# Modulation computed by blocks of 128 channels, the first two projection tiles summed channel block by channel block, and later roundings of the output weights

## The reference

```python
shift, scale, gate = jnp.split(jax.nn.silu(mod) @ p['ada_w'] + p['ada_b'], 3, -1)
h = rms_norm(x, p['g_pre']) * (1.0 + scale) + shift
z = h @ p['w_in']                      # 1024 -> 4096
... three branches: gated conv, conv module, bidirectional RWKV-7 scan
out = jnp.concatenate([ya, yb, yc], -1) @ p['w_out']
x = x + gate * rms_norm(out, p['g_post'])
```

## Time and profile before

| | us |
|---|---|
| median of 3 runs (lowest, highest) | 1085.96 (1084.84, 1086.45) |
| profiled execution | 1087.09 |
| its span | 1085.3 |

### The profile page before, as it was taken

The page is one execution under the profiler, slowest core; times in us unless marked ns, Lnnn a source line. Parts: engine busy times, 40 slices in busy tenths (PEclk is TensorE's granted clock), DMA queues, the critical chain, the costliest instruction groups (busy, mean ns, idle before and its releaser), DMA issues. The chain is left out here.

```text
span 1085.3 us, 31987 instructions
## 1 busy us (share of the span) xinstructions
PE 1005.1 (93%) x14375; PEld 907.3 (84%) x14375; DVE 641.6 (59%) x952; ACT 426.4 (39%) x708; POOL 409.3 (38%) x372
## 2 busy tenths in 40 slices
PE   5699999999999999994699999999999998899997
PEld 3399999999989888983699999999999997566685
DVE  5351059776457302245688888888888885546532
ACT  5361102100124332222355655666555665434311
POOL 8111112311205312322446555566676665512200
PEclk9699999999999999996699999999999999999999
DMA  9711422111122110000000000000000004421331
GB/s 356 268 37 62 178 84 79 40 39 39 39 83 81 42 39 1 1 1 11 1 4 4 4 4 4 4 4 5 4 4 4 4 4 159 135 109 35 121 117 59
DMA packets 30564, 61.46 MB, mean 57 GB/s; under 512 B 3368, under 2 KB 21972, under 8 KB 29276
## 3 DMA queue, kind: packets, MB, share of 16 engines
q1 hardware_dynamic: 30428, 59.42, 15.5%
HBM read 49.68 MB, written 9.73 MB: 55 GB/s over the span
## 5 line engine op out<-in xcount | busy, mean ns | idle before, releaser
L681 PE MATMUL ps<-input_rounded,weights_rounded 128*128 128x386 f32 x768 | 264.0, 344 | 4.1 <-DVE input_rest L788 2.8
L683 PE MATMUL ps<-input_rounded,weights_rest 128*128 128x386 f32 x768 | 260.7, 339 | 0.0
L682 PE MATMUL ps<-input_rest,weights_rounded 128*128 128x386 f32 x768 | 260.4, 339 | 0.0
L1464 POOL TENSOR_TENSOR arena<-arena,lvl 128x512 f32<-128x512 f32 x108 | 138.8, 1300 | 78.2 <-ACT arena L1372 46.4
L470 POOL TENSOR_TENSOR weights_rest<-arena,weights_rounded 128x2048 fp32r<-128x2048 f32 x16 | 75.8, 4737 | 211.2 <-ACT weights_rounded L515 211.2
L681 PEld LDWEIGHTS ps<-input_rounded,weights_rounded 128*128 128x128 f32 x768 | 145.1, 189 | 10.9 <-issue 7.5
L682 PEld LDWEIGHTS ps<-input_rest,weights_rounded 128*128 128x128 f32 x768 | 145.3, 189 | 0.5
L683 PEld LDWEIGHTS ps<-input_rounded,weights_rest 128*128 128x128 f32 x768 | 145.4, 189 | 0.0
L1157 PE MATMUL ps<-arena 64*64 64x64 f32 x2880 | 107.0, 225 | 18.1 <-issue 14.6
L1157 PEld LDWEIGHTS ps<-arena 64*64 64x64 f32 x2880 | 95.2, 138 | 23.8 <-issue 17.1
L1167 PE MATMUL ps<-arena 64*64 64x64 f32 x2880 | 104.9, 223 | 5.4 <-DVE arena L1595 4.1
(11 more groups left out here) (247 smaller groups left out, 1700.8 us busy)
## 6 DMA issues: line engine op xcount, KB each, us to landing
arena<-in_w_in SPq DMA_DIRECT2D x16, 1024.0 KB, 5.2
arena<-in_ada_w SPq DMA_DIRECT2D x7, 1024.0 KB, 5.3
mix_scratch<-zc SPq DMA_DIRECT2D x4, 1158.0 KB, 9.7
out<-arena SPq DMA_DIRECT2D x9, 512.0 KB, 2.6
zc<-in_x_sample SPq DMA_DIRECT2D x4, 1024.0 KB, 9.1
hT<-in_ada_w SPq DMA_DIRECT2D x4, 1024.0 KB, 12.1
zc<-in_w_out SPq DMA_DIRECT2D x4, 1024.0 KB, 8.6
arena<-in_x_sample SPq DMA_DIRECT2D x8, 512.0 KB, 3.7
```

The source lines that it names most:

```text
L681: pe.matmul(o, w_hi[:, k, cut], hi_of_h[:, k, cols_b], start=(k == 0), stop=False)
L682: pe.matmul(o, w_hi[:, k, cut], lo_of_h[k][:, cols_b], start=False, stop=False)
L683: last = pe.matmul(o, w_lo[:, k, cut], hi_of_h[:, k, cols_b], start=False, stop=(k == KT - 1))
L1464: pool.tensor_tensor(Um[l % 3], UT, lvl[:, l, :].unsqueeze(1).to_broadcast([P, 2 * PAIRS, C]), ALU.mult).then_inc(q_um[l], 1)
```

## The change

- `load_ada(k)` now loads output block k: the 128 shift columns and the 128 scale columns of all 1024 input rows, as two DMAs with runs of 512 bytes. `modulate(k)` sums all eight input blocks for these 256 outputs at once (eight matmuls of 256 columns in four partition groups), `copy_rows(k)` on ScalarE copies the result from PSUM, and `turn(k)` on TensorE sums the four groups and transposes them by two matmuls with a selection matrix. The bias is added per channel in `scale_and_shift(k)`; shift and scale biases are loaded with the small vectors.
- SP's order: x, vectors, ada block 0, first weights, ada blocks 1 to 7, gate rows, LoRA weights.
- The roots take mean and epsilon in the activation, without VectorE, and follow each group's squares. Tile 5 is evicted by VectorE, tile 4 by ScalarE.
- Tiles 0 and 1 sum over channel blocks: for the first six (`TOGETHER`) channel blocks, both tiles and all three column blocks in six banks of PSUM, with the modulation of block k + 2 ahead of block k's products; then the last two channel blocks for tile 0, then for tile 1. `full`, `round_inputs` and `rest` go by channel block, VectorE taking the first two column blocks and ScalarE modulating the third.
- The first weights are rounded in four pieces, the first after block 0's rows, the others behind the first channel blocks; the second weights behind channel block 5. GpSimd makes the rests of the four pieces, and builds the small constants early.
- `round_w_out`: part 0 goes to the place that part 1 had, 1 to that of 2, 2 to that of 3, and 3 behind `copy_y(n3, 4)` of the next step, the last one.

The core of the diff (lines shifted left):

```diff
 GROUPS = ((0,), (1, 2), (3, 4), (5, 6), (7, 8))
-H_CUTS = [(n, k) for n in range(NB) for k in range(KT)]
-EVICT_BY = [1, 1, 1, 1, 1, 0, 0, 0, 0]
+EVICT_BY = [1, 1, 1, 1, 0, 1, 0, 0, 0]
 X_SLOTS = 3
 BY_ACT = 2
+TOGETHER = KT - 2
+CHUNKS = 4
+CHUNK = PIECE // CHUNKS
...
 def load_ada(k):
-    sp.dma_start(ada_at[k], ada_w[0, k * P:(k + 1) * P, 0:2048]).then_inc(s_al[k], 16)
+    for s in range(2):
+        at = D_MODEL * s + P * k
+        sp.dma_start(ada_at[k].rearrange("p (m s n) -> p s m n", m=KT, s=2)[:, s],
+                     ada_w[0, :, at:at + P].rearrange("(m p) n -> p m n", p=P)).then_inc(s_al[k], 16)
...
+load_ada(0)
+load_z(0)
+for k in range(1, KT):
+    load_ada(k)
...
+def early():
+    for n, e in enumerate((RMS_EPS, LN_EPS, KK_EPS, GN_EPS)):
+        pool.memset(epst[:, n:n + 1], e)
+    link(pool.memset(select, 0.0))
+    for b in range(4):
+        link(pool.affine_select(out=select, in_=select, compare_op=ALU.not_equal, fill=1.0, base=-32 * b,
+                                pattern=[[-1, 2]], channel_multiplier=1))
+    for v in (kkT, lo2):
+        for a in (0, TS - 2, W - 2):
+            last = pool.memset(v[:, 0:4, a:a + 2], 0.0)
+    last.then_inc(s_const, 1)
...
+def split_first(c):
+    cut = slice(CHUNK * c, CHUNK * c + CHUNK)
+    pool.wait_ge(s_wh0, c + 1)
+    pool.tensor_tensor(w_rest[:, 0, cut], ring[:, 0, cut], w_round[:, 0, cut].bitcast(F32),
+                       ALU.subtract).then_inc(s_wr0, 1)
...
 def deviation(g):
     a, b = GROUPS[g][0], GROUPS[g][-1] + 1
-    act.wait_ge(s_ms, g + 1)
-    act.activation(ss[:, a:b], ss[:, a:b], ACT.Sqrt).then_inc(s_sd, 1)
+    act.wait_ge(s_ss, b)
+    if g == 0:
+        act.wait_ge(s_const, 2)
+    act.activation(ss[:, a:b], ss[:, a:b], ACT.Sqrt, bias=epst[:, 0:1], scale=1.0 / D_MODEL).then_inc(s_sd, 1)
...
+def copy_rows(k):
+    act.wait_ge(s_wu, k + 1)
+    if k >= 2:
+        act.wait_ge(s_at, k - 1)
+    half = slice(256 * (k % 2), 256 * (k % 2) + 256)
+    act.activation(row[:, half], ps[:, 6, half], ACT.Copy).then_inc(s_row, 1)
+
+def round_inputs(k):
+    act.wait_ge(s_hf, k + 1)
+    act.activation(hi_of_h[:, k, 0:BY_DVE_END], lo_full[k][:, 0:BY_DVE_END], ACT.Copy).then_inc(s_ha, 1)
+    if k == 0:
+        act.wait_ge(s_xc[0], evicted(0, 8))
+    act.activation(lo_full[k][:, BY_DVE_END:W - 2], lo_full[k][:, BY_DVE_END:W - 2], ACT.Identity,
+                   bias=shf[:, k, 1:2], scale=scl[:, k, 1:2]).then_inc(s_hfa, 1)
+    act.wait_ge(s_hfa, k + 1)
+    act.activation(hi_of_h[:, k, BY_DVE_END:W], lo_full[k][:, BY_DVE_END:W], ACT.Copy).then_inc(s_ha, 1)
+
+evict(4)
+copy_rows(0)
+evict(6)
+round_first(0)
+evict(7)
+evict(8)
+for k in range(KT):
+    round_inputs(k)
+    if k == 0:
+        copy_rows(1)
+        round_first(1)
+    if k + 2 < KT:
+        copy_rows(k + 2)
+    if k < 2:
+        round_first(k + 2)
+    if k == KT - 3:
+        round_weights(1)
...
 def modulate(k):
-    pe.wait_ge(s_al[k], 16)
-    for b in range(4):
-        last = pe.matmul(ps[32 * b:32 * b + 2, 0, :], mods[:, k, :], ada_at[k][:, 512 * b:512 * b + 512],
-                         start=(k == 0), stop=(k == KT - 1))
+    pe.wait_ge(s_al[k], 32)
+    if k:
+        pe.wait_ge(s_row, k)
+    half = slice(256 * (k % 2), 256 * (k % 2) + 256)
+    for m in range(KT):
+        b = 32 * (m % 4)
+        last = pe.matmul(ps[b:b + 2, 6, half], mods[:, m, :], ada_at[k][:, 256 * m:256 * m + 256],
+                         start=(m < 4), stop=(m >= 4))
     last.then_inc(s_wu, 1)
...
+def turn(k):
+    pe.wait_ge(s_row, k + 1)
+    if k:
+        pe.wait_ge(s_sc, k)
+    else:
+        pe.wait_ge(s_vc, 3)
+    for s in range(2):
+        at = 256 * (k % 2) + P * s
+        last = pe.matmul(turned(k)[:, 2 * s:2 * s + 2], row[:, at:at + P], select, start=True, stop=True)
+    last.then_inc(s_at, 1)
...
+for i in range(5):
+    transpose_x(i)
+pe.wait_ge(s_vec, 16 * (len(VEC_ROWS) - 1))
+pe.transpose(ps[:, 7, 0:N_ROWS], va[0:N_ROWS, :], eye[0:N_ROWS, 0:N_ROWS]).then_inc(s_vt, 1)
+pe.transpose(ps[:, 7, P:P + N_CB], vb[0:N_CB, :], eye[0:N_CB, 0:N_CB]).then_inc(s_vt, 1)
+for i in range(5, 7):
     transpose_x(i)
 pe.wait_ge(s_pclear, 1)
-for k in range(5):
-    transpose_x(k + 4)
-    modulate(k)
-pe.wait_ge(s_vec, 16 * (len(VEC_ROWS) - 1))
-pe.transpose(ps[:, 7, 0:N_VEC], va[0:N_VEC, :], eye[0:N_VEC, 0:N_VEC]).then_inc(s_vt, 1)
-pe.transpose(ps[:, 7, P:P + N_CB], vb[0:N_CB, :], eye[0:N_CB, 0:N_CB]).then_inc(s_vt, 1)
-for k in range(5, KT):
-    modulate(k)
-pe.wait_ge(s_row, 1)
-pe.wait_ge(s_xc[EVICT_BY[6]], evicted(EVICT_BY[6], 6))
-for m in range(4):
-    last = pe.transpose(ps[:, 1, P * m:P * m + P], row[:, P * m:P * m + P], eye[:, :])
-last.then_inc(s_at, 1)
+pe.wait_ge(s_const, 2)
+modulate(0)
+transpose_x(7)
+turn(0)
+transpose_x(8)
+modulate(1)
+turn(1)
...
+    return last
+
+pe.wait_ge(s_xc[0], evicted(0, 8))
+pe.wait_ge(s_xc[1], evicted(1, 8))
+for k in range(TOGETHER):
+    if k < TOGETHER - 1:
+        modulate(k + 2)
+    pe.wait_ge(s_wr0, k // 2 + 1)
+    pe.wait_ge(s_hs, 2 * k + 1)
+    for b in range(BY_ACT):
+        for j in range(2):
+            products(j, b, [k])
+    if k < TOGETHER - 1:
+        turn(k + 2)
+    if k == TOGETHER - 2:
+        modulate(KT - 1)
+    if k == TOGETHER - 1:
+        turn(KT - 1)
+    pe.wait_ge(s_hs, 2 * k + 2)
+    for j in range(2):
+        products(j, BY_ACT, [k])
+for j in range(2):
+    for k in range(TOGETHER, KT):
+        pe.wait_ge(s_wr0, CHUNKS)
+        pe.wait_ge(s_hs, 2 * k + 2)
+        for b in range(NB):
+            last = products(j, b, [k])
+    last.then_inc(s_z, 1)
...
+def scale_and_shift(k):
+    dve.wait_ge(s_at, k + 1)
+    dve.tensor_scalar(shf[:, k, :], turned(k)[:, 0:2], col("b_shift", k), None, ALU.add)
+    dve.tensor_scalar(scl[:, k, :], turned(k)[:, 2:4], col("b_scale", k), col("g_pre", k),
+                      ALU.add, ALU.mult).then_inc(s_sc, 1)
+
+def full(k):
+    dve.wait_ge(s_sc, k + 1)
+    dve.tensor_scalar(lo_full[k][:, TP:TP + SEQ], lo_full[k][:, TP:TP + SEQ], scl[:, k, 0:1],
+                      shf[:, k, 0:1], ALU.mult, ALU.add)
+    dve.tensor_scalar(lo_full[k][:, TS:BY_DVE_END], lo_full[k][:, TS:BY_DVE_END], scl[:, k, 1:2],
+                      shf[:, k, 1:2], ALU.mult, ALU.add).then_inc(s_hf, 1)
+
+def rest(k):
+    for part, cut in enumerate((slice(0, BY_DVE_END), slice(BY_DVE_END, W))):
+        dve.wait_ge(s_ha, 2 * k + part + 1)
+        dve.tensor_tensor(lo_of_h[k][:, cut], lo_full[k][:, cut], hi_of_h[:, k, cut].bitcast(F32),
+                          ALU.subtract).then_inc(s_hs, 1)
+
+link(dve.tensor_scalar(cols("b_scale"), cols("b_scale"), 1.0, None, ALU.add))
+dve.wait_ge(s_xc[0], evicted(0, 4))
+dve.wait_ge(s_xc[1], evicted(1, 5))
+for k in range(KT + 1):
+    if k < KT:
+        scale_and_shift(k)
+        full(k)
+    if k:
+        rest(k - 1)
...
-    if n2 == N - 1:
-        round_w_out(0)
     if 0 <= n3 < N:
         copy_y(n3, 4)
+    if n3 == N - 1:
+        round_w_out(3)
...
     if n2 == N - 1:
-        round_w_out(1)
+        round_w_out(0)
...
     if n2 == N - 1:
-        round_w_out(2)
+        round_w_out(1)
...
     if n2 == N - 1:
-        round_w_out(3)
+        round_w_out(2)
```

More of the change, by code:

```diff
@@ L219, in hybrid_step_kernel @@
         spare = rT.rearrange("p a w -> p (a w)")
-        row, adab = spare[:, 0:512], spare[:, 512:1024]
+        row = spare[:, 0:512]
+        select = small[:, 34:36]
         hflat = hT[:, :, :].rearrange("p k w -> p (k w)")
@@ L419, in link @@
                     pool.wait_ge(s_pool, n_pool[0])
-                pool.memset(adab, 0.0)
                 pool.memset(grow, 0.0)
@@ L434, in _ @@
                         pool.tensor_copy(eye[:, :], blocks[:, 0, :]).then_inc(s_const, 1)
+                        early()
                 link(pool.tensor_copy(heads[:, :], blocks[:, 6, :]))
@@ L445, in _, with split_rest @@
                                             base=base, pattern=[[sign, P]], channel_multiplier=-sign))
+                def split_first(c):
[3 more added lines that the diff above has]
+                                       ALU.subtract).then_inc(s_wr0, 1)
+                def split_rest(p):
+                    at = slot_of("z", p)
+                    pool.wait_ge(s_wh, p)
+                    pool.tensor_tensor(w_rest[:, at, :], ring[:, at, :], w_round[:, p % 2, :].bitcast(F32),
+                                       ALU.subtract).then_inc(s_wo1, 1)
+                for c in range(CHUNKS):
+                    split_first(c)
                 for d in range(2):
@@ L504, in _ @@
                         act.activation(junk, xtok[:, i, :], ACT.Square, accum_out=ss[:, i:i + 1]).then_inc(s_ss, 1)
[L505 to L510 removed]
+                    deviation(g)
                 def round_weights(p):
@@ L663, in kk_norm, with products @@
                                   start=True, stop=True).then_inc(s_ks, 1)
-                pe.wait_ge(s_const, 3)
-                pe.wait_ge(s_w2, 32)
```

(32 more changed lines are left out.)

147 lines of the change are left out of this document (41 added, 106 removed).

## The result

The changed kernel takes 1088.21 us (median of 20 runs, 1085.75 to 1089.35) where the kernel before took 1086.05 on the same chip (20 runs): ratio 1.002, 95% interval 1.0013 to 1.0027. It is slower by 2.2 us; forecast was 9 faster, and no rival named this way of losing. The profiled execution has a span of 1087.1, 1.8 above the one before, and where these 1.8 lie can be read from it.

The account below looks back on a forecast made before the run. TensorE's unbroken matmul string was taken to bound the kernel, so an earlier end of tile 1 moves everything behind it. 1087.09 - 7.9 (front) - 1.2 (back) = 1078.0, less 1.1 to the runs' median: 1076.9 us; range 1073.5 to 1082.5.

Parts of the forecast that it names:

- front: Everything up to ScalarE's read of tile 1, forecast 7.9 us earlier, 69.2 against 77.1, range 6.7 to 9.8.
- first product: TensorE's first projection matmul of tiles 0 and 1, forecast at 34.2 us against 48.3 before.
- block 1: Start of channel block 1's products in the loop over channel blocks, forecast at 38.85 us.
- block 5: Start of channel block 5, after five loop steps of 4.65 us, forecast at 57.4 us.
- joint end: Products of channel blocks 6 and 7 for tiles 0 and 1, forecast from 62.6 us: 36 products, 6.34, plus 0.3 waiting.
- tile 1 read: ScalarE's read of output tile 1 after its last matmuls, forecast at 69.2 us against 77.1 before.
- what I cost at nothing: Loads, roundings and GpSimd work around the first two tiles, claimed to be hidden and to add 0 us.
- GpSimd's rest of it: GpSimd's subtraction for the second weights, 4.5 us, claimed done at 64.5 and due at 69, so free.
- the clock falls in the new gap: Rival: TensorE idles from 28.4 to 31.6 us and its clock halves for a while, costing 2.5: 1079.4 us, chance 0.34.
- A step: One of five passes of the loop over channel blocks, forecast 4.65 us, with VectorE's chain later than TensorE by 0.3.
- The back: New order of the last weights' roundings at the scan's end, forecast to gain 1.2 us, bounds 0 to 1.4.
- The loads: Ada loads in 512 byte runs: 26 ns a packet, 3.4 us a block, claimed hidden until about 4.4 a block.

Follow-up runs that it names:

- late split: The changed kernel with GpSimd's rest of the second weights put behind VectorE's modulation of channel block 7 by one more wait: 1082.51 us, ratio 0.9963.
- warm gap: The late split kernel with 29 unread transposes of the unit matrix filling TensorE's waits from 26 to 32.5 us: 1087.88 us, ratio 1.0026.
- the warm gap and no hold: The changed kernel with the 29 idle transposes and the second weights' rest in two halves behind VectorE's last rest of the inputs: 1082.68 us, ratio 0.9974.

## Why the prediction was wrong

Five marks of the front, forecast, measured and late by: first product 34.2, 34.27, 0.1; block 1 38.85, 40.52, 1.7; block 5 57.4, 60.88, 3.5; joint end 62.6, 69.51, 6.9; tile 1 read 69.2, 78.36, 9.2.

- *The step that failed* stands in the list of what I cost at nothing: "GpSimd's rest of it (4.5) is due at 69 and done at 64.5". I asked when it is due and not whom it stands beside. Its own times had the two side by side, the subtraction from 60.0 to 64.5, block 7's modulation and the last rests from 59.5 to 62.6. In the run it was done at 67.41 and stood beside the modulation of block 7, which I gave 0.8: 3.4 late at the joint end, 3.1 of it one instruction (3.44 against 0.35). The trace of before had the sign, which I had not looked for. There VectorE normalises two x tiles in 2.17 beside a GpSimd subtraction and in 1.41 without one:

```profile
13.70 2.17 DVE L740 TENSOR_SCALAR zc<-zc,small 128x1024 f32<-128x1024 f32 x2
...
21.37 1.41 DVE L740 TENSOR_SCALAR zc<-zc,small 128x1024 f32<-128x1024 f32 x2
```

```profile
13.92 1.41 POOL L439 TENSOR_TENSOR lvl<-arena 64x384 f32<-64x384 f32 x1
```

- *The stop's second price.* The joint end took 8.85 instead of 6.6: 2.25 at half clock. Hold and clock together are 5.7, and the late split gives back 5.7 of the time. The rival "the clock falls in the new gap" was priced at 2.5 for one fall, with 0.34; it happened there (about 1.2, step 0 taking 6.25 against (60.88 - 40.52) / 4 = 5.09 for the other four; 1.4 by the warm gap's trace, which reads tile 1 at 71.12 against the late split's 72.55) and again in a gap I had not foreseen.
- *A term mis-sized.* A step was put at 4.65 and took 5.09. The terms as the prediction writes them make 4.76 (2.11 + 0.25 + 2.4), so 0.1 of it was lost in the adding. In the step from 45.69 the products are 2.19 (2.11 forecast), turn and hop 0.53 (0.39), scale and shift 0.45 (0.22 and a hop), modulation 0.79 (0.8), rest and hop 1.1 (1.0). Five steps make 2.2. Turned into the middle of the products, the turn brought 4.8, which shows that VectorE's chain set it.
- *The back* (forecast 1.2, bounds 0 to 1.4): the copy and the update went 2.6 and 1.3 earlier as worked out, but TensorE's next product was stopped by "issue" beside the loads of w_out. Measured gain: none beyond the runs' spread. The trace of before has a stop of 0.67 behind the same 20 matmuls, which the prediction passed over, when it was the next wait:

```profile
911.80 0.56 PE L1157 MATMUL ps<-arena 64*64 64x64 f32 x12 [0.67 <-issue]
```

- *Right by luck:* the first product. turn(1) came at 30.00 and not at 31.6, and VectorE's rests of block 0 ran from 32.33 to 33.75, so the products could have begun at about 33.4, as they do with the warm gap and no hold (33.45). TensorE was then still in the modulation of block 2, which had waited 1.44 for its load and took 1.89 at half clock, until 34.27. Two errors made up for each other.
- *The loads* were a little under-sized. An ada block's packets took 30 ns (9253 packets with 109.5% of the 16 engines' time in 24 to 40 us: 1.095 x 16 x 16 us / 9253) where I took 26. TensorE waited for them at 28.07, which ScalarE's work on block 0 covered until 29.58, and at 32.45, which nothing covered; from the second step on they cost nothing. The second weights were rounded at 62.80 and not by 59.7, with 0.94 of ScalarE's wait.

## What to carry to other kernels

Cover is not only time: ask of each moved instruction of GpSimd which VectorE instructions on SBUF it will stand beside, and put it behind the last one that TensorE waits for, by a wait, not by a margin of 0.2 us. A stop in front of a string of matmuls can be paid twice, here once in itself (3.4) and once in the clock (2.25). And where a wait is taken away, look at the small "issue" idle beside it: it may be what ends last next.

## What the runs showed of the hardware

- VectorE and GpSimd hold each other on SBUF data, whoever starts first: a tensor_scalar of 128 columns took 3.44 instead of 0.35, two-input subtractions 7.01 instead of 2.77, and with VectorE first GpSimd's took 7.07 instead of 4.54. Small tensor_scalars that read PSUM ran in their 0.22 and 0.27 in the middle of GpSimd's instruction.
- The Trainium skill, "SBUF — State Buffer", section "Who interferes with whom", says just this: the pair of ports that VectorE and GpSimd share goes to whoever issues first for a whole instruction, and VectorE takes it for two SBUF inputs (against a GpSimd instruction that reads SBUF) or in its two-port modes, which tensor_scalar can enter. This case agrees in all three rows above. It was the rule that spoke against this change, and the prediction left it out.
- The hold can last for more than one instruction. When VectorE's instructions follow each other without a gap, GpSimd waits for several in a row (2.5 us for four rests), and a gap of 0.23 was enough for VectorE to lose the turn.
- TensorE's stops by "issue" of 0.6 to 2.7 us at the scan's end moved with the 4 MB of w_out's loads (some 410 GB/s), and stand at a place counted in its instructions: 29 instructions put in at the front moved one by 29. Each ended 2.4 to 2.6 us after a late 16 KB packet of the instruction queue had started.
